# A hybrid attention and RWKV backbone on one core: VectorE's order in the RWKV loop body and the place of SyncE's stores of y

## The chip, the cores and the metric
The program runs on one core of a Trainium2 chip. The metric is device time in microseconds (us) of one execution. The kernel before takes 5541.4 us (median of 3 runs, 5534.21 to 5553.46). All data is float32, but for one small helper product of the attention phase.

## The reference, cut to what matters
The program computes two layers over 2048 latent and 256 context tokens of width 1024. Layer 0 is latent attention beside Fourier mixing, layer 1 is bidirectional RWKV-7 time mixing. The change lies in layer 1 alone, whose recurrence is this (16 heads of 64, two directions `d`):

```
decay = exp(-exp(-softplus(-w_raw) - 0.5));  a = sigmoid(a0 + ad @ a2)
kk = normalised k * k_k;      k_dir = k * (1 + (a - 1) * k_a)
step: sa = S kk;   S = S * decay - sa (kk * a)^T + v k_dir^T;   y = S r
out  = group_norm(y_fwd + y_bwd) + (sum(r * k_dir * r_k)) * v, times a SiLU gate, times w_out
```

The kernel does the recurrence in chunks of 64 tokens. Inside a chunk the steps are a triangular system. Its 64x64 matrix is split in 16x16 blocks: the diagonal blocks are inverted by back substitution, and the rest follows from matrix products.

## The kernel before, in words
`program` runs phases one after the other: modulation, projections, attention, Fourier mixing and their merge (the first 3600 us of the profiled execution), then `rwkv` (L1632 to L2349), then `merge1` with group norm and the output projection.

`rwkv` has 72 items (`NBODY`): 8 pairs of heads times 9 groups of 256 tokens, in this order. One item carries both directions and both heads of a pair, with 4 chunks of 64. The work on an item is spread over six loop bodies, so that one body `n` works on several items at once: the recurrence proper on item n (`step_begin`, `step_sa`, `step_end`, four times), the off-diagonal part of the inverse on item n+1 (`far_p`, `first_order`, `second_w`, `higher_orders`), the inverses' way back from memory on item n+2, scores and block inversion on item n+3, and rates, decays, keys and queries on item n+4, whose inputs are loaded a body earlier. All loops are unrolled. Each engine has its own instruction stream with an order written out by hand in its function `body`; engines meet by semaphores only. An instruction stream stands still at a wait until the semaphore is there, and all that is behind it stands too.

SyncE (SP) issues every DMA of this phase, on one hardware queue. For body n it has in order `store_bonus(n+3)` (2 DMAs), `load(n+5)` (4, and 4 more at the first group of a pair), `keep_products(n+3)` (4 stores of the masked scores), `keep_inverses(n+2)` (1 store of the inverted diagonal blocks), `gather(n+3)` (2 loads of the diagonal blocks of what `keep_products` has stored), `spread(n+2)` (8 loads of the inverses into XB) and `store_y(n)` (4 stores). `gather` waits for the stores of `keep_products` to land; `keep_inverses` waits for GpSimd's last copy; `spread` waits for the store of `keep_inverses` to land.

GpSimd (POOL) has only `invert(n+3)`: one copy into place (L1864), a memset, 28 small multiply and add instructions in a chain (L1870, L1872), four copies out (L1881). It begins when `gather` has landed.

TensorE (PE) begins body n with `bonus(n+3)` (L1915) and runs the four steps of the recurrence with the other products between them. Behind step 2's `step_begin` stand `far_p` (L1957, needs XB from `spread`), `step_sa`, `far_p`, `step_end`, then `first_order` (L1970, needs Pm from VectorE's `blocks`, L2279), step 3 and `higher_orders` (L1988).

VectorE (DVE) runs `bonus`, `decay_of_chunks`, `parameters`, `carry` (L2264) and `decayed` (L2257) for each step, `masks` (L2272), `sums` (L2218 to L2221), `keys` (L2226 to L2230: t1, kd, b0, q), `blocks` (L2279), `add_orders` (L2291), `queries` (L2236, L2237: two products into AR) and `weights` (L2242, L2243: Kc, Bc) in the order of L2303 to L2347. ScalarE copies PSUM results and computes the exponentials; its `take_y` (L2154) writes y into one of two buffers and waits at a body's first step for the stores of two items earlier.

Of the kernel before, what the change touches and what calls it, by code (L numbers as in the profile page):

```python
# [24 lines left out]
ALU = mybir.AluOpType  # L25
# [1606 lines left out]
def rwkv(nc, sem, keep, A, W):  # L1632

    with ExitStack() as stack:
        core = Core(nc, stack, "rw")
        NBODY = PAIRS * NG
# [5 lines left out]
        zin = core.sb("zin", [P, 2, 2, 4, GT])  # L1642
# [3 lines left out]
        cur = core.sb("cur", [P, 7])  # L1646
# [4 lines left out]
        ee = core.sb("ee", [P, 2, 2, GT])  # L1651
        cs, en, t1, kd, b0, q, bv = (core.sb(n, [P, 2, GT]) for n in ("cs", "en", "t1", "kd", "b0", "q", "bv"))
# [28 lines left out]
        ep_done, ar_done, kb_done = (sem(f"rw_{n}") for n in ("ep_en", "ar", "kb"))  # L1681
# [9 lines left out]
        x_mm, x_out, p_mm, p_out, xt_mm, xt_out = ([sem(f"rw_{n}{d}") for d in range(2)] for n in (  # L1691
            "x_mm", "x_out", "p_mm", "p_out", "xt_mm", "xt_out"))
# [31 lines left out]
        def tokens(m, d):  # L1724

            return m.group * GT if d == 0 else ((NG - m.group) % NG) * GT

        def span(first, size):
            return slice(first, first + size) if isinstance(first, int) else bass.ds(first, size)
# [4 lines left out]
        def bodies(one):  # L1734

            for n in range(1 - KEEP - 2, NBODY):
                one(At(n), [0 <= n + k < NBODY for k in range(KEEP + 2)])

        with nc.Block() as block:
            @block.sync  # L1740
            def _(sp):
# [19 lines left out]
                def whole(scratch, d, h, turned=0):  # L1761
                    first = NCH * (4 * turned + 2 * d + h)
                    return W[scratch][first:first + NCH, 0:C * C].rearrange("c (s t) -> s c t", t=C)

                def diagonal(scratch):
                    return W[scratch].rearrange("q (b x) -> (q b) x", b=NSUB)[:, 0:SUB * C].rearrange("u (i t) -> u i t", t=C)[:, :, 0:SUB]
# [21 lines left out]
                def keep_inverses(m):  # L1788

                    sp.wait_ge(inv_done, 4 * m.n + 4)  # L1790
                    if m.since(1):
                        sp.wait_ge(xb_l, 16 * 8 * m.n)
                    sp.dma_start(diagonal("inverses"), g_out[:].rearrange("u (i j) -> u i j", j=SUB)).then_inc(i_st, 16)

                def spread(m):

                    sp.wait_ge(i_st, 16 * (m.n + 1))
                    if m.since(2):
                        for d in range(2):
                            sp.wait_ge(xt_mm[d], 2 * m.n - 3)  # L1800
                    for turned in (1, 0):
                        for d in range(2):
                            for h, (rows, _) in enumerate(HEADS2):
                                sp.dma_start(XB[rows, m.two, turned, d], whole("inverses", d, h, turned)).then_inc(xb_l, 16)

                def store_y(n):
                    sp.wait_ge(y_out, 4 * n.n + 4)
                    for d in range(2):
                        for h, (rows, _) in enumerate(HEADS2):
                            dst = W["y"][d, span(tokens(n, d), GT), span(n.pair * P + HP * h, HP)]  # L1810
                            sp.dma_start(dst.rearrange("(c t) v -> t c v", t=C),
                                         ysb[rows, GT * (2 * n.two + d):GT * (2 * n.two + d) + GT].rearrange("t (c v) -> t c v", c=NCH)).then_inc(y_st[n.two][d], 16)
# [18 lines left out]
                def body(n, has):  # L1831
                    if has[3]:
                        store_bonus(n.on(3))
                    if has[5] and n.since(-3):
                        load(n.on(5))
                    if has[3]:
                        keep_products(n.on(3))
                    if has[2]:
                        keep_inverses(n.on(2))
                    if has[3]:  # L1840
                        gather(n.on(3))
                    if has[2]:
                        spread(n.on(2))
                    if has[0]:
                        store_y(n)

                bodies(body)
                sp.wait_ge(bv_st, 32 * NBODY)
                for both in y_st:
                    for d in range(2):  # L1850
# [344 lines left out]
            def _(v):  # L2195
# [24 lines left out]
                    nc.vector.tensor_tensor_scan(cs[:, 0, :], reset[:, 0, :], ee[:, 0, 0, :], 0.0, ALU.mult, ALU.add).then_inc(cs_done, 1)  # L2220
                    nc.vector.tensor_tensor_scan(cs[:, 1, ::-1], reset[:, 1, ::-1], ee[:, 0, 1, ::-1], 0.0, ALU.mult, ALU.add).then_inc(cs_done, 1)  # L2221

                def keys(m, link):
                    s = m.two
                    v.wait_ge(in_l[s], inputs_loaded(m))
                    link(nc.vector.tensor_scalar(t1[:], ee[:, 1], cur[:, 4:5], cur[:, 5:6], ALU.mult, ALU.add))  # L2226
                    link(nc.vector.tensor_tensor(kd[:], t1[:], zin[:, s, :, 0, :], ALU.mult))
                    link(nc.vector.scalar_tensor_tensor(out=b0[:], in0=ee[:, 1], scalar=-1.0, in1=zin[:, s, :, 1, :], op0=ALU.mult, op1=ALU.mult))
                    v.wait_ge(bon_mm, m.n)
                    nc.vector.scalar_tensor_tensor(out=q[:], in0=zin[:, s, :, 2, :], scalar=cur[:, 6:7], in1=kd[:],  # L2230
                                                   op0=ALU.mult, op1=ALU.mult).then_inc(q_done, 1)

                def queries(m):
                    s = m.two
                    v.wait_ge(ep_done, m.n + 1)
                    nc.vector.tensor_tensor(AR[:, m.six, :, :, 1, :], decayed_to(True), by_chunk(zin[:, s, :, 2, :]), ALU.mult).then_inc(ar_done, 1)  # L2236
                    nc.vector.tensor_tensor(AR[:, m.six, :, :, 0, :], decayed_to(False), by_chunk(zin[:, s, :, 1, :]), ALU.mult).then_inc(ar_done, 1)  # L2237

                def weights(m):

                    v.wait_ge(sc_mm, 4 * m.n)
                    nc.vector.tensor_tensor(Kc[:], kd[:], en[:], ALU.mult)  # L2242
                    nc.vector.tensor_tensor(Bc[:], b0[:], en[:], ALU.mult).then_inc(kb_done, 1)  # L2243
# [38 lines left out]
                def add_orders(m, d, which):  # L2282

                    v.wait_ge(xt_mm[d], 2 * m.n + which + 1)
                    if which == 0:
                        v.wait_ge(xb_l, 16 * 8 * (m.n + 1))
                    else:
                        v.wait_ge(xt_out[d], 2 * m.n + 1)
                    grown = XT[:, m.two, d].rearrange("p c t -> p (c t)")
                    less = grown if which else XB[:, m.two, 0, d].rearrange("p c t -> p (c t)")  # L2290
                    nc.vector.tensor_tensor(grown, bank[XT_AT[d]][:, 0:GT], less, ALU.add).then_inc(xt_out[d], 1)  # L2291
# [11 lines left out]
                def body(n, has):  # L2303
                    m, k, l = n.on(1), n.on(3), n.on(4)
                    link = Link(v, dch, EL * l.n)
                    if has[3]:
                        bonus(k)
                        decay_of_chunks(k)
                    if has[4]:
                        parameters(l)  # L2310
                    if has[0]:
                        carry(n, 0)
                        decayed(n, 1)
                    if has[3]:
                        masks(k, 0, 0)
                    if has[4]:
                        sums(l, link)
                    if has[3]:
                        masks(k, 0, 1)
                    if has[0]:  # L2320
                        carry(n, 1)
                        decayed(n, 2)
                    if has[3]:
                        for d in range(2):
                            masks(k, 1, d)
                    if has[4]:
                        keys(l, link)
                    if has[1]:
                        for d in range(2):
                            blocks(m, d)  # L2330
                    if has[0]:
                        carry(n, 2)
                        decayed(n, 3)
                    if has[1]:
                        for d in range(2):
                            add_orders(m, d, 0)
                    if has[4]:
                        queries(l)
                    if has[0]:
                        carry(n, 3)  # L2340
                        if has[1]:
                            decayed(m, 0)
                    if has[4]:
                        weights(l)
                    if has[1]:
                        for d in range(2):
                            add_orders(m, d, 1)  # L2347

                bodies(body)  # L2349


# [333 lines left out]
```

## Time and profile before
The profiled execution took 5547.19 us, its span in the trace is 5545.2 us.

| what | value |
|---|---|
| median of 3 runs | 5541.4 us |
| profiled execution, own time | 5547.19 us |
| its span | 5545.2 us |
| rwkv phase in it | about 3600 to 5262 us |
| busy over the span, PE / DVE / ACT / POOL | 92% / 50% / 28% / 24% |
| PE busy, 3720 to 5180 us | 1345.54 of 1460 us |
| mean granted TensorE clock | 0.971 of full speed |

A timeline row has the start in us, the duration in us, the engine, the line, the operation with its operands and, in brackets, how long the engine was idle before it and what released it. `SPq` rows are DMA issues: the duration is SP's time for the issue, and not the transfer's. A row with x8 stands for eight instructions in a row.

### The profile page before, as it was taken

The numbers are of one execution on the slowest core, as the hardware profiler recorded it, in microseconds if no ns is written. First come the engines' busy times: TensorE is split into PE (matmuls) and PEld (weight loads), VectorE is DVE, ScalarE is ACT, GpSimd is POOL, SyncE is SP. The second block draws the span as 40 slices with busy tenths as digits, with TensorE's granted clock in tenths as the row PEclk, the third lists the DMA queues.
The fourth block names the chain that finished last, engine by engine and source line by source line (L and its number), as shares of the span: only waits on it lengthen the run. The fifth ranks groups of instructions, "written<-read, shape, count | busy, mean of one in ns | idle before, by whom it ended". The sixth has DMA issues, their size and how long they took to land. (4 is left out here: it accounts for less than half of the span.)

```text
span 5545.2 us, 133161 instructions
## 1 busy us (share of the span) xinstructions
PE 5083.7 (92%) x53870; PEld 3081.3 (56%) x53870; DVE 2745.9 (50%) x4947; ACT 1544.6 (28%) x3503; POOL 1342.8 (24%) x2817
## 2 busy tenths in 40 slices
PE   7899997999999987999999999879999899999879
PEld 2566663333333323444444444468888888888734
DVE  0233343666666651221232222267777666777566
ACT  0111211443434430232211212123333333333222
POOL 0011011222222220000000000045555555555333
PEclk9999997999999998999999999989999999999989
DMA  6212222000000007332121121155555555555485
GB/s 248 74 61 69 64 64 68 4 22 23 22 23 22 22 32 284 123 117 57 57 69 65 57 69 60 50 135 128 131 128 134 129 132 129 132 133 131 86 275 174
DMA packets 926936, 527.19 MB, mean 95 GB/s; under 512 B 661312, under 2 KB 879040, under 8 KB 919360
## 3 DMA queue, kind: packets, MB, share of 16 engines
q1 hardware_dynamic: 926400, 519.62, 33.3%
q8 instruction: 387, 6.34, 0.5%
q14 instruction: 149, 1.22, 0.1%
HBM read 330.98 MB, written 188.49 MB: 94 GB/s over the span
## 5 line engine op out<-in xcount | busy, mean ns | idle before, releaser
L1534 PE MATMUL p_bU<-keep_hT,p_slab 128*128 128x512 f32 (+1 forms) x2592 | 1029.3, 559 | 12.8 <-DMA p_slab<-in_o_w_in_dram 7.3
L1534 PEld LDWEIGHTS p_bU<-keep_hT,p_slab 128*128 128x128 f32 x2592 | 493.4, 191 | 543.6 <-issue 512.1
L883 PE MATMUL at_bS<-at_qT,at_kT 97*64 97x512 f32 (+1 forms) x2368 | 602.4, 598 | 7.2 <-issue 6.6
L1015 DVE TENSOR_REDUCE at_mx<-at_bM 128x1 f32<-128x512 f32 (+1 forms) x656 | 400.6, 629 | 354.0 <-PE at_bM L849 351.0
L978 ACT ACTIVATE at_pT<-at_bS 128x512 f32<-128x512 f32 (+1 forms) x592 | 346.8, 591 | 462.3 <-PE at_bS L883 383.9
L1606 DVE SCALAR_TENSOR_TENSOR p_z<-p_u,p_shift,p_z 128x2306 f32<-128x2306 f32 x26 | 68.2, 2621 | 769.9 <-ACT p_z L1564 769.9
L1872 POOL TENSOR_TENSOR rw_g_at<-rw_g_at,rw_g_prod 64x14 f32<-64x14 f32 (+6 forms) x1008 | 333.4, 331 | 79.0
L1870 POOL TENSOR_TENSOR rw_g_prod<-rw_g_at 64x14 f32<-64x14 f32 (+6 forms) x1008 | 324.4, 322 | 79.1
L2264 DVE SCALAR_TENSOR_TENSOR rw_S<-rw_bank,rw_dec,rw_Sdec 128x64 f32<-128x64 f32 x576 | 136.8, 279 | 382.7 <-PE rw_bank L2039 382.4
L883 PEld LDWEIGHTS at_bS<-at_qT,at_kT 97*64 97x64 f32 x2368 | 161.0, 138 | 267.2 <-issue 214.9
L902 PE MATMUL at_bO<-at_pT,at_va 128*64 128x512 f32 x1152 | 300.5, 600 | 0.0
L806 POOL TENSOR_TENSOR at_sum_pool<-at_sum_pool,at_pT 128x512 f32<-128x512 f32 x128 | 192.8, 1506 | 433.4 <-ACT at_pT L978 422.0
L1036 DVE TENSOR_TENSOR at_sum_vector<-at_sum_vector,at_pT 128x512 f32<-128x512 f32 x320 | 276.1, 863 | 13.1 <-ACT at_pT L978 9.7
L1883 POOL MEMSET rw_zeros<- 128x1040 f32 x1 | 1.0, 964 | 1104.7 <-POOLq L2604 1104.7
L1324 PE MATMUL m_bY<-m_w,m_mT 128*128 128x512 f32 x576 | 251.3, 594 | 0.0
L422 PE MATMUL p_bG<-keep_w_in,p_hT 128*128 128x512 f32 x576 | 250.1, 592 | 0.0
L1558 ACT COPY p_u<-p_bU 128x512 f32<-128x512 f32 (+1 forms) x130 | 69.6, 542 | 643.3 <-PE p_bU L1534 629.3
L849 PE MATMUL at_bM<-at_kTb,at_qTb 96*64 96x512 bf16 (+1 forms) x1312 | 224.5, 365 | 11.9 <-DVE at_mx L1015 10.9
L2495 PE MATMUL m_bY<-m_w,m_oT 128*128 128x512 f32 x512 | 223.5, 595 | 0.0
L373 POOL TENSOR_TENSOR p_hr<-p_hms,p_half 128x8 f32<-128x8 f32 x36 | 58.9, 1636 | 576.6 <-DVE p_hms L558 576.6
L849 PEld LDWEIGHTS at_bM<-at_kTb,at_qTb 96*64 96x64 bf16 x1312 | 75.4, 109 | 219.4 <-issue 136.8
L2154 ACT COPY rw_ysb<-rw_bank 128x128 f32<-128x128 f32 x288 | 77.6, 269 | 387.3 <-DVE rw_S L2264 386.4
(261 smaller groups left out, 9506.2 us busy)
## 6 DMA issues: line engine op xcount, KB each, us to landing
rw_zin<-scratch_heads SPq DMA_DIRECT2D x144, 512.0 KB, 4.7
rw_XB<-scratch_inverses SPq DMA_DIRECT2D x576, 64.0 KB, 2.6
mod_w<-in_ada_w_dram SPq DMA_DIRECT2D x4, 6144.0 KB, 18.1
scratch_heads<-p_z SPq DMA_DIRECT2D x24, 1024.0 KB, 4.9
rw_lin<-scratch_lora SPq DMA_DIRECT2D x144, 128.0 KB, 5.2
scratch_bv<-rw_bv SPq DMA_DIRECT2D x144, 128.0 KB, 2.0
scratch_products<-rw_NB SPq DMA_DIRECT2D x288, 64.0 KB, 4.0
scratch_y<-rw_ysb SPq DMA_DIRECT2D x288, 64.0 KB, 2.2
```

The costliest lines, as they stand in the source:

```text
L422: last = pe.matmul(bG[:, j, :], hT[:, s, k, :], w_in[:, k, E_G0 + 512 * j:E_G0 + 512 * (j + 1)], start=(k == 0), stop=(k == KD - 1))
L849: last = pe.matmul(bM[rows, (FIRST_ITEM[b] + i) % 2, 0:n], qTb[:, s, q0 + VH * x:q0 + VH * x + VH], kTb[:, s, c:c + n], start=True, stop=True)
L883: last = pe.matmul(bS[rows, g % 3, 0:nq * P], kT[:, s, k * P + VH * x:k * P + VH * x + VH], qT[:, s, q0 * P:(q0 + nq) * P], start=True, st ...
L902: last = pe.matmul(out[rows, 0:nq * P], va[:, s, 2 * pair + x, :], pT[:, (g + x) % SLOTS, 0:nq * P], start=(pair == 0), stop=(pair == nk / ...
L978: nc.scalar.activation(pT[:, g % SLOTS, 0:n], bS[:, g % 3, 0:n], ACT.Exp, scale=SCALE).then_inc(exp_done, 1)
L1015: nc.vector.tensor_reduce(mx[:, j, piece:piece + 1], bM[:, (FIRST_ITEM[b] + i) % 2, 0:n], AX.X, ALU.max).then_inc(max_red, 1)
L1036: nc.vector.tensor_tensor(acc, acc, tile, ALU.add).then_inc(added[False], 1)
L1324: last = pe.matmul(bY[:, j, :], mT[:, s, k, :], w[:, k, j * 512:(j + 1) * 512], start=(k == 0), stop=(k == KD - 1))
L1534: last = pe.matmul(bU[:, n % 4, 0:w], slab[:, i, k, :], hT[:, k, tok:tok + w], start=(k == 0), stop=(k == KD - 1))
L1870: link(nc.gpsimd.tensor_tensor(prod, N[:, k + 1:, k:k + 1].broadcast_to([2 * half, rows, k]), N[:, k:k + 1, 0:k].broadcast_to([2 * half, r ...
L1872: link(nc.gpsimd.tensor_tensor(below, below, prod, ALU.add))
L2495: last = pe.matmul(bY[:, 2 * s + j, :], oT[:, s, k, :], w[:, k, j * 512:(j + 1) * 512], start=(k == 0), stop=(k == KD - 1))
```

## The change
On SP, `store_y` of body n's own item at the end of the body becomes `store_y` of the item before, issued between `keep_inverses` and `gather`; one `store_y` for the last item stands behind the loop. `spread` now waits for VectorE's `add_orders` of two items earlier (`xt_out`) where it waited for TensorE's product behind it (`xt_mm`).

On VectorE, `keys` is cut in three. `key_factors` (t1) stays between `masks` and `blocks`. `new_keys` (kd, q) and `bonus_weights` (b0) move behind the first `add_orders`, where `queries` stood. `queries` moves to the end of the body. `weights` waits for `ep_done` itself. No operation is added or taken away.

```diff
@@ SP: spread
-                            sp.wait_ge(xt_mm[d], 2 * m.n - 3)
+                            sp.wait_ge(xt_out[d], 2 * m.n - 3)
@@ SP: body
                         keep_inverses(n.on(2))
+                    if has[0] and n.since(1):
+                        store_y(n.on(-1))
                     if has[3]:
                         gather(n.on(3))
                     if has[2]:
                         spread(n.on(2))
-                    if has[0]:
-                        store_y(n)
 
                 bodies(body)
+                store_y(At(NBODY - 1))
@@ DVE: keys is cut in three
-                def keys(m, link):
+                def key_factors(m, link):
+                    link(nc.vector.tensor_scalar(t1[:], ee[:, 1], cur[:, 4:5], cur[:, 5:6], ALU.mult, ALU.add))
+
+                def new_keys(m, link):
                     s = m.two
                     v.wait_ge(in_l[s], inputs_loaded(m))
-                    link(nc.vector.tensor_scalar(t1[:], ee[:, 1], cur[:, 4:5], cur[:, 5:6], ALU.mult, ALU.add))
                     link(nc.vector.tensor_tensor(kd[:], t1[:], zin[:, s, :, 0, :], ALU.mult))
-                    link(nc.vector.scalar_tensor_tensor(out=b0[:], in0=ee[:, 1], scalar=-1.0, in1=zin[:, s, :, 1, :], op0=ALU.mult, op1=ALU.mult))
                     v.wait_ge(bon_mm, m.n)
                     nc.vector.scalar_tensor_tensor(out=q[:], in0=zin[:, s, :, 2, :], scalar=cur[:, 6:7], in1=kd[:],
                                                    op0=ALU.mult, op1=ALU.mult).then_inc(q_done, 1)
+
+                def bonus_weights(m, link):
+                    s = m.two
+                    link(nc.vector.scalar_tensor_tensor(out=b0[:], in0=ee[:, 1], scalar=-1.0, in1=zin[:, s, :, 1, :], op0=ALU.mult, op1=ALU.mult))
@@ DVE: weights
+                    v.wait_ge(ep_done, m.n + 1)
                     v.wait_ge(sc_mm, 4 * m.n)
@@ DVE: body
                     if has[4]:
-                        keys(l, link)
+                        key_factors(l, link)
                     if has[1]:
                         for d in range(2):
                             blocks(m, d)
...
                     if has[4]:
-                        queries(l)
+                        new_keys(l, link)
+                        bonus_weights(l, link)
                     if has[0]:
                         carry(n, 3)
...
                     if has[1]:
                         for d in range(2):
                             add_orders(m, d, 1)
+                    if has[4]:
+                        queries(l)
```

## Rows read from the trace of the kernel before
**Rows 1.** TensorE's waits, 3720 to 4480 us: line waited for, total us, times, longest
```profile
PE rw_bank L1970 <- DVE rw_Pm L2279: 31.5, 28, 1.5
PE rw_bank L1957 <- DMA rw_XB<-scratch_inverses: 20.1, 14, 3.2
```
**Rows 2.** The same, 4480 to 5180 us
```profile
PE rw_bank L1970 <- DVE rw_Pm L2279: 49.7, 31, 2.2
```
**Rows 3.** The waits of SP's DMA queue, 3720 to 4480 us
```profile
SPq L1786 <- DMA scratch_products<-rw_NB: 76.3, 34, 4.3
SPq L1793 <- POOL rw_g_out L1881: 18.4, 16, 2.6
```
**Rows 4.** Timeline of SP, a late body: from one gather to the next
```profile
4504.54 0.33 SPq L1786 DMA_DIRECT2D rw_g_in<-scratch_products  x1
...
4511.69 3.48 SPq L1811 DMA_DIRECT2D scratch_y<-rw_ysb  x4
...
4519.09 2.62 SPq L1778 DMA_DIRECT2D scratch_products<-rw_NB  x4
4521.81 1.56 SPq L1793 DMA_DIRECT2D scratch_inverses<-rw_g_out  x1
4525.47 0.33 SPq L1786 DMA_DIRECT2D rw_g_in<-scratch_products  x1
```
**Rows 5.** Timeline of SP: the fourth gather of the phase
```profile
3700.34 0.84 SPq L1786 DMA_DIRECT2D rw_g_in<-scratch_products  x1
```
**Rows 6.** Line 1786's instructions: min/median/max ns, first and last start
```profile
L1786 SPq DMA_DIRECT2D rw_g_in<-scratch_products x72: 325/332/1189, 3642.8 to 5209.5; - x72
```
**Rows 7.** POOL by line, 3720 to 4480 us: busy us, mean ns, idle before
```profile
L1864 POOL COPY rw_g_at<-rw_g_in 32x256 f32<-32x256 f32 x34 | 14.3, 421 | 236.1 <-DMA rw_g_at<-scratch_products 236.1
```
**Rows 8.** The same, 4480 to 5180 us
```profile
L1864 POOL COPY rw_g_at<-rw_g_in 32x256 f32<-32x256 f32 x32 | 15.2, 475 | 263.1 <-DMA rw_g_at<-scratch_products 263.1
```
**Rows 9.** Timeline, the late body of rows 4: POOL, one VectorE scan, TensorE's far_p
```profile
4507.67 0.39 POOL L1864 COPY rw_g_at<-rw_g_in 32x256 f32<-32x256 f32 x1 [8.19 <-DMA rw_g_at<-scratch_products]
...
4514.46 0.27 POOL L1870 TENSOR_TENSOR rw_g_prod<-rw_g_at 64x50 f32<-64x50 f32 x1
...
4514.81 0.61 POOL L1872 TENSOR_TENSOR rw_g_at<-rw_g_at,rw_g_prod 64x50 f32<-64x50 f32 x1
...
4515.32 0.69 DVE L2220 TENSOR_TENSOR_SCAN rw_cs<-rw_reset,rw_ee 128x256 f32<-128x256 f32 x1
...
4518.59 2.27 POOL L1881 COPY rw_g_out<-rw_g_at 32x256 f32<-32x256 f32 x4
...
4519.33 0.60 PEld L1957 LDWEIGHTS rw_bank<-rw_XB,rw_NB 64*64 64x64 f32 x16
```
**Rows 10.** Timeline of SP, an early body: gather, stores of y
```profile
4279.36 0.33 SPq L1786 DMA_DIRECT2D rw_g_in<-scratch_products  x1
...
4287.74 2.59 SPq L1811 DMA_DIRECT2D scratch_y<-rw_ysb  x4
...
4299.73 0.38 SPq L1793 DMA_DIRECT2D scratch_inverses<-rw_g_out  x1
4301.52 0.78 SPq L1786 DMA_DIRECT2D rw_g_in<-scratch_products  x1
```
**Rows 11.** Timeline of POOL, the same body
```profile
4283.30 0.39 POOL L1864 COPY rw_g_at<-rw_g_in 32x256 f32<-32x256 f32 x1 [7.63 <-DMA rw_g_at<-scratch_products]
...
4296.81 2.90 POOL L1881 COPY rw_g_out<-rw_g_at 32x256 f32<-32x256 f32 x4
```
**Rows 12.** Timeline, TensorE's far_p in that body
```profile
4289.47 0.68 PE L1957 MATMUL rw_bank<-rw_XB,rw_NB 64*64 64x64 f32 x16 [0.73 <-DMA rw_XB<-scratch_inverses]
```
**Rows 13.** Timeline of VectorE, the first of blocks in the late body
```profile
4522.83 0.75 DVE L2279 TENSOR_TENSOR rw_Pm<-rw_bank,rw_far 128x256 f32<-128x256 f32 x2
```
**Rows 14.** Timeline of TensorE, from first_order to the next body's begin
```profile
4501.20 1.15 PE L1970 MATMUL rw_bank<-rw_XB,rw_Pm 64*64 64x64 f32 x32 [1.98 <-DVE rw_Pm L2279]
...
4506.20 1.13 PE L1915 MATMUL rw_bank<-rw_q,rw_same 128*128 128x512 f32 x2
```

## The prediction
> **What bounds the kernel now.** I read the share of busy time first, and it misleads: TensorE is busy 92% of the span, and in the stretch 3720 to 5180 us, which is the steady part of the RWKV loop, 1345.54 of 1460 us. A reader would take the loop as bound by TensorE with some 8% of idle time. So the second view is TensorE's waits in that stretch. Two lines hold nearly all of them: `first_order` (L1970) waits for VectorE's Pm, 31.5 + 49.7 us, and `far_p` (L1957) waits for the DMA that brings XB, 20.1 us [rows 1, 2]. Together 101.3 us over some 66 bodies, 1.53 us each.
>
> The third view is SP's own timeline, since XB comes from there. How long is a body? The 72 gathers run from 3642.8 to 5209.5 us [rows 6]; from the fourth, at 3700.34 us [rows 5], to the last are 68 bodies in 1509.2 us: 22.19 us each. In one such body, from 4504.54 to 4525.47 us, SP issues back to back: stores of y end where those of the bonus begin, and so on to the products, which end at 4521.71. Only in front of `gather` does it stand still, after the store of the inverses [rows 4]. The waits of SP's queue say so too: 76.3 us in 34 bodies, 2.24 each, for the stored products to land, and GpSimd's result is late in 16 of the 34, 18.4 us in all [rows 3]. So SP itself is almost full, and it is a second bound at about TensorE's period.
>
> The fourth view is GpSimd, whose 24% of busy time looks harmless. It is one link of a ring that nothing can pipeline: gather(n+3) lands, GpSimd inverts, SP stores the result, and only then SP issues the next gather, since the order on SP says so. In the late body gather is issued at 4504.54, GpSimd starts at 4507.67 and ends at 4520.86 (4518.59 + 2.27): 3.13 us and then 13.19 us [rows 4, 9]. In an early body it starts at 4283.30, 3.94 us behind the gather of 4279.36, and ends at 4299.71: 16.41 us for the same 35 instructions; SP stores at 4299.73, 0.02 us later [rows 10, 11]. By groups, GpSimd's idle time in front of its first copy is 236.1/34 = 6.9 us a body in the early stretch and 263.1/32 = 8.2 us in the late one [rows 7, 8]; with 760/34 and 700/32 us for a body it works 15.4 and 13.7 us.
>
> **Why GpSimd's time varies.** One small multiply of 64x50 takes 0.27 us, the add of the same shape begun 0.35 us later takes 0.61 us, and a scan of VectorE over operands in SBUF runs from 4515.32 for 0.69 us at the same time as GpSimd's next ones [rows 9]. Over the trace, GpSimd's instructions stretch while VectorE runs operations whose operands all lie in SBUF (`sums`, t1, kd, b0, q, Kc, Bc, both of AR, `decayed`) and not while VectorE reads PSUM (`masks`, `blocks`, `carry`, `add_orders`). In GpSimd's stretch of the late body I count 4.0 us of such VectorE work (the first in it is `decayed` at 4512.73, the last kd, cut off at 4520.86), in that of the early body 8.6 us (from L2218 at 4283.66 to Bc at 4297.67, 15 instructions). So (16.41 - 13.19)/(8.6 - 4.0) = 0.70 us of GpSimd per us of it. What sets the count is the phase: `far_p` starts 14.8 us behind the gather in the late body (4519.33) and 10.1 us in the early one (4289.47), where TensorE had waited 0.73 us for XB [rows 9, 12].
>
> **The change part by part.**
> (a) *VectorE, keys behind blocks.* In the late body `blocks` starts at 4522.83, 3.5 us behind `far_p` [rows 9, 13], because kd, b0 and q stand ahead of it. In the new order t1 is over 1.05 us behind the start of `far_p`, `blocks` follows, and the first Pm is there before `step_end`, so TensorE's 31.5 + 49.7 us go [rows 1, 2]: up to 81.2/66 = 1.23 us a body. What is late next: the second product of `far_p` and `step_end`, which run to 2.0 us behind `far_p`'s start; nothing in between waits for VectorE.
> (b) *kd, q, b0 in the place of queries.* Three operations of about 0.7 us for two (the scan of 0.69 us is the nearest size [rows 9]): 0.8 us more in front of the fourth `carry`. There VectorE had been idle 1.3 to 2.4 us for TensorE's last product of the step; I charge 0, and if that cover fails 0.3 us a body.
> (c) *queries last.* Its 1.4 us now stand in front of the next body's `bonus`, where VectorE had waited 3.2 us ahead of the first `carry`. AR and bv are wanted 6.6 us into the body; ScalarE's `rates` wants AR 5.5 us in, and it is there some 3.5 us in. Cost 0, upper end 0.3 us.
> (d) *The two waits.* `weights` waits for exponentials that are more than 5 us old; `spread` for sums a body old. Behind `spread`'s wait on SP stand only the next body's issues. 0.
> (e) *Stores of y on SP.* 3.48 us of issue in the late body, 2.59 in the early one [rows 4, 10]; I take 3.1 with 0.1 between. They fill the 2.24 us in front of `gather` and also the 0.5 us in which `spread` waited. SP's own sum falls from 22.2 to about 19.5 us. But they now stand in GpSimd's ring: between the inverses' store and the gather. `take_y` wants y of two items before; in the tight phase that lands about when it is asked for, some 0.6 us late at worst, under TensorE's wait for XB.
>
> Three periods are left. TensorE: 22.19 - 1.53 = 20.7 us; the sum of one body is the same, 5.0 us from `first_order` to the next body [rows 14], 13.1 from there to `far_p` [rows 9, 14] and 2.0 back to `first_order`: 20.1 at full clock. SP: 19.5. The ring: 3.3 (gather to GpSimd's start; 3.13 and 3.94 above) + P + 0.03 + 0.4 (store of inverses) + 3.2 (y) = 6.9 + P. P depends on the phase. At the start `far_p` is 14 us behind the gather: queries have left GpSimd's stretch, so P is about 14.0 and the ring 20.9, plus 0.2 for a worse landing: 21.1. That is longer than TensorE's 20.7, so TensorE gains on the ring and `far_p` moves towards the gather, which brings kd, q, b0 and both weights into GpSimd's stretch. It stops where TensorE waits for XB, 9 to 10 us behind the gather. There the stretch holds half of `sums` (1.0 us), t1 0.6, kd, q, b0 2.2, Kc and Bc 1.4, a part of queries 0.4 and three `decayed` 0.9: 6.5 us, P = 13.19 + 0.70 x (6.5 - 4.0) = 14.9, and the ring 22.0 with 0.2 for the landing. So in the end the loop runs at the ring's pace, 0.2 us under today's. I give the drift 16 bodies: 16 x (22.19 - 21.1) = 17 us and 52 x (22.19 - 22.0) = 10 us. Sum: -27 us. The profiled execution's own time, 5547.19, would be 5520; it lies 5.8 us above the median of 5541.4, so against that I forecast **5514 us**. P has ends of 13.2 and 16.4 from rows 9 and 11, the issue of y 2.6 and 3.5 from rows 10 and 4: rings of 19.7 to 23.9.
>
> The Trainium skill, SBUF — State Buffer, section "SBUF: two separate sides", says that a VectorE operation with two inputs in SBUF and a GpSimd operation that reads SBUF exclude each other for a whole instruction and do not share bandwidth. The two bodies agree in kind (0.27 against 0.61 us), with 0.70 us lost per us of overlap. It speaks against this change, because it lets the ring grow where one counts SP's time alone: with a full 1.0 us per us, P would be 15.7 and the steady ring 22.8 us, slower than today's.
>
> **The rivals.**
> *Ring too long (slower).* The place is SP between the inverses' store and `gather`; the price is y's issue plus a GpSimd that is stretched more than by my count, or a gather that lands behind y's packets. It decides from P + landing over 18.6 us. For it: P of 16.4 was seen at just this phase [rows 11]. Against: queries, 1.4 us, have left that stretch. With P at 15.9 and 22.9 us for 60 bodies: 60 x 0.75 - 8 x 1.1 = +36, so 5577 us.
> *TensorE's pace (faster by more).* The ring stays near its short phase, with P at 13.5 to 13.8. For it: the late stretch keeps 13.7 us for 32 bodies [rows 8], and any lull of TensorE's clock moves the phase back. Against: the ring's 21.1 is then still longer than 20.7 by my count. 20.8 us for 68 bodies: -95, so 5446 us.
> *Nothing to be had.* The ring in its locked phase has just today's period, and the short phase lasts few bodies: 5541 us. That SP is nearly full today could be a follower's slack and no bound; then only the ring's 22.2 counts.
>
> **How the numbers follow.** Forecast 0.43, its own range 5490 to 5540; ring too long 0.23; TensorE's pace 0.18; nothing 0.16. About 0.3%, 17 us, is what a measurement of this kernel can tell from no change: under 5525 the forecast's case has two thirds of its chance (0.29) and TensorE's pace all of it, which gives 0.48 for faster; the rest of the forecast's (0.12) and of the third rival's (0.14) give 0.26 for the same, 0.26 is slower. The range of 5452 to 5580 leaves out somewhat more than half of the lower case and under half of the upper one.
>
> **What would show it.** Right: TensorE's wait of L1970 for Pm is gone; a wait of L1957 for XB stands in most bodies from the middle of the loop on, about 1 us each; SP waits for GpSimd (L1793) in nearly every body and for the products in hardly any; the gather follows the stores of y at once; GpSimd works about 15 us a body and idles 7. Wrong: L1793's wait stays rare and L1957's absent (then TensorE sets the pace, near 5446), or bodies of more than 22.5 us with GpSimd above 15.5 us (the slower case); a Pm wait that stays, or a new wait of TensorE for AR, Kc or q, would refute (a), (b) or (c).

## The result: slower by 0.5%, and the profile after
The changed kernel takes 5566.9 us (median of 6 runs, 5560.4 to 5570.3) against 5538.9 us before; the ratio is 1.005, with a 95% interval of 1.0039 to 1.0061. The forecast was 5514. The profiled execution took 5566.7 us, its span is 5564.7 us, and from the fourth gather (3700.05 us) to the last (5229.7 us) it is 1529.7 us where it was 1509.2: these 68 bodies are 20 us longer, about the whole of the difference. Of the rivals it is the slower one, "ring too long".

TensorE's waits of the kernel after, 3720 to 4480 us (answers to [rows 1]):
```profile
PE rw_bank L1958 <- DMA rw_XB<-scratch_inverses: 27.0, 22, 2.2
PE rw_bank L2011 <- ACT rw_ysb L2155: 21.3, 13, 2.6
```
The wait for Pm (31.5 us) is gone, as part (a) had it, and nothing was won: TensorE waits for XB instead, and for ScalarE's copy of y, which stands still until the stores of y two items earlier have landed (34.3 us in 17 of ScalarE's waits in this stretch).

SP's waits in the same stretch (to [rows 3]):
```profile
SPq L1793 <- POOL rw_g_out L1882: 97.3, 30, 5.2
SPq L1811 <- ACT rw_ysb L2155: 4.8, 5, 2.1
```
The 76.3 us for the stored products are gone too. SP now waits for GpSimd in 30 of 34 bodies where it did in 16. An engine that waits is no bound, so SP has been relieved, and the ring with GpSimd in it sets the pace. The second row is no wait: at the store issued at 4329.62 us, one of these five, ScalarE's last copy of that y had ended at 4305.95; the issue itself took so long. One turn of the ring, SP (to [rows 4, 10]):
```profile
4288.79 0.55 SPq L1786 DMA_DIRECT2D rw_g_in<-scratch_products  x1
...
4300.27 2.66 SPq L1778 DMA_DIRECT2D scratch_products<-rw_NB  x4
4308.24 0.38 SPq L1793 DMA_DIRECT2D scratch_inverses<-rw_g_out  x1
4308.66 3.61 SPq L1811 DMA_DIRECT2D scratch_y<-rw_ysb  x4
4312.37 0.55 SPq L1786 DMA_DIRECT2D rw_g_in<-scratch_products  x1
```
and GpSimd and TensorE in it (to [rows 11, 12]):
```profile
4292.91 0.39 POOL L1865 COPY rw_g_at<-rw_g_in 32x256 f32<-32x256 f32 x1 [8.38 <-DMA rw_g_at<-scratch_products]
...
4305.12 3.09 POOL L1882 COPY rw_g_out<-rw_g_at 32x256 f32<-32x256 f32 x4
```
```profile
4298.74 0.68 PE L1958 MATMUL rw_bank<-rw_XB,rw_NB 64*64 64x64 f32 x16
```
SP has its products out at 4302.93 and stands until 4308.24. Landing 4.12, GpSimd 15.30, wake-up 0.03, store of the inverses 0.38, y and its gaps 3.75: 23.58 us, one of the longer turns. `far_p` starts 9.95 us behind the gather.

The same sum can be drawn up for every kernel below. These are means over the gathers 5 to 70 of each profiled execution, in us: the period from gather to gather; gather to GpSimd's start; GpSimd's work P; from its end to the issue of the inverses' store; that issue; from there to the next gather; and how far `far_p` starts behind the gather.

```
kernel                          period landing    P   to SP  issue  to gather  far_p behind
before                           22.19   3.27  14.67   1.22   0.60     2.42        13.7
changed                          22.53   3.67  14.61   0.06   0.41     3.78        10.1
VectorE's order alone            21.88   3.20  14.81   0.93   0.59     2.34         9.9
SP's order alone (at 5608 us)    23.16   3.65  15.38   0.06   0.38     3.69        10.0
y ahead of the inverses          21.35   4.36  14.28   1.93   0.64     0.13        12.6
pad in SBUF                      22.72   3.77  14.78   0.07   0.41     3.68        10.0
pad with PSUM                    22.41   3.62  14.39   0.15   0.42     3.83        10.4
y split around gather            21.41   3.69  14.14   0.28   0.53     2.78        12.8
y ahead, bonus behind gather     20.73   4.48  13.92   1.49   0.68     0.15        15.6
products ahead of load           23.17   7.09  13.68   1.76   0.54     0.11        17.0
that of 20.73, VectorE's old     21.94   4.27  13.96   2.92   0.68     0.11        18.5
```
"To SP" tells ring from SP: near 0.03 us SP stood waiting for GpSimd and the ring is the bound; above a microsecond GpSimd was done and SP was busy, or stood, with something else. The row of SP's order alone is of an execution of 5608 us, and of that kernel more is said below. A ratio counts only the executions within 1.5% of the fastest of their kernel, which leaves out four of SP's order alone, all above 5600 us.

Against the kernel before GpSimd's own time is the same (14.61 and 14.67). What grew is the way from the inverses' store to `gather`, 1.36 us, where y's issue stands in place of the wait for the products, and the landing, 0.40 us; the 1.22 us of slack behind GpSimd's end is used up.

### The profile page after: what moved, and what is told of

It is laid out like the page before. It is cut to its first block and busy times, and to the rows that moved or that the text cites. A ratio compares the mean times of both kernels' runs of the same rounds, so it can differ in the third digit from the quotient of the medians.

```text
span 5564.7 us, 133236 instructions
## 1 busy us (share of the span) xinstructions
PE 5090.7 (91%) x53870; PEld 3083.8 (55%) x53870; DVE 2762.1 (50%) x4947; ACT 1545.1 (28%) x3503; POOL 1337.0 (24%) x2817
## 5 line engine op out<-in xcount | busy, mean ns | idle before, releaser
L1871 POOL TENSOR_TENSOR rw_g_prod<-rw_g_at 64x14 f32<-64x14 f32 (+6 forms) x1008 | 308.1, 306 | 79.1
L1882 POOL COPY rw_g_out<-rw_g_at 32x256 f32<-32x256 f32 x288 | 192.9, 670 | 17.8
## 6 DMA issues: line engine op xcount, KB each, us to landing
mod_w<-in_ada_w_dram SPq DMA_DIRECT2D x4, 6144.0 KB, 18.3
```

Of the source, the lines that this page charges most:

```text
L1871: link(nc.gpsimd.tensor_tensor(prod, N[:, k + 1:, k:k + 1].broadcast_to([2 * half, rows, k]), N[:, k:k + 1, 0:k].broadcast_to([2 * half, r ...
```

## The experiments
**Either part alone.** First the diff's VectorE part with the old SP order, then SP's part with VectorE's old order.

> VectorE's new order alone; on SP the stores of y stay at the end of the body. Ring theory (the new order on SP puts the issue of y into the ring gather, GpSimd, store of the inverses, next gather): without y the ring is about 18.5 us a body and no bound; SP, full at 22.2 us before, keeps its sum, so the time stays within 0.4% of before (5520 to 5555), TensorE's waits move from L1970 (Pm) to L1958 (XB). Rival, VectorE's order is what costs: slower than before by the 0.5% of the change, some 5565. Rival, TensorE was the bound: 1.2 us a body less, 5455.

Measured: 5525.8 us, 0.9972 of before (0.996 to 0.9983). The waits of TensorE are for XB, as expected (3720 to 5180 us):
```profile
PE rw_bank L1957 <- DMA rw_XB<-scratch_inverses: 73.2, 49, 3.5
```
VectorE's order is not what costs, and TensorE was not the bound: with Pm's wait gone SP's turn, its waits for its own stores in it, sets the pace, at 21.88 us. `far_p` is 9.9 us behind the gather here too, and GpSimd is no faster than in the changed kernel (14.81 us): the tight phase costs little as long as y is out of the ring.

> SP's new order alone; VectorE keeps the old one, with keys ahead of blocks and queries ahead of the fourth carry. Ring theory: slower than before, and by more than the whole change, since queries (1.4 us of VectorE work in SBUF) lie in GpSimd's stretch too: GpSimd 15 to 15.5 us a body, period 23.0, 5580 to 5610. Rival, VectorE's order is what costs: about 5540 or faster.

> The kernel with SP's new order alone once more, for another profile: in five of its seven executions it took 5523 to 5530 us, in two 5608 and 5611, and the profiled one was of the second kind (far_p 10.0 us behind gather, GpSimd 15.4 us a body). Phase theory: an execution of the first kind has far_p 12 us or more behind gather, GpSimd below 14.7 us, TensorE waiting for Pm rather than for XB, and a period of about 22.0. Rival, the second kind is a disturbance from outside: the same phase and the same GpSimd time, with other stretches (PE clock, DMA landing) longer.

> The kernel with SP's new order alone, timed again. Two levels were seen, 5525 and 5610 us. If they are two phases of one ring in which an execution settles by itself, both come again in some mixture and hardly anything between; the profiled one shows far_p 10 us behind gather if it is near 5610, and 12 us or more if it is near 5525. If the first series' 5525 was chance, all are near 5610.

The first expectation was missed in five executions of seven, and what came is the best view of the mechanism. The first series had executions of 5523 to 5530 us (five) and of 5608 and 5611; the ratio of the five is 0.9967 (0.9955 to 0.998). The profiled one is that of 5608 us, and it is as expected: GpSimd 15.38 us, period 23.16. The second time the one execution took 5616, with `far_p` 10.2 us behind the gather, GpSimd 15.43 us and a period of 23.21: the same again. The third series had 5522, 5529, 5530, 5533, 5535, 5569, 5583, 5586, 5622 and 5623 us; without the last two the ratio is 0.9989 (0.9964 to 1.0015), no change that this can tell. Low and high times come again, but three lie between, and the trace of one of these says why. The granted clock does not tell them apart (0.971 at 5530 and 5586 us, 0.970 and 0.971 at 5608 and 5611). In the profiled one of 5586 us the phase changes half-way. Its gather of 3803.98 us and the `far_p` behind it:
```profile
3803.98 0.60 SPq L1786 DMA_DIRECT2D rw_g_in<-scratch_products  x1
```
```profile
3821.60 0.68 PE L1958 MATMUL rw_bank<-rw_XB,rw_NB 64*64 64x64 f32 x16
```
17.6 us. The gather of 4285.00 us and its `far_p`:
```profile
4285.00 0.55 SPq L1786 DMA_DIRECT2D rw_g_in<-scratch_products  x1
```
```profile
4294.22 0.68 PE L1958 MATMUL rw_bank<-rw_XB,rw_NB 64*64 64x64 f32 x16 [0.27 <-DMA rw_XB<-scratch_inverses]
```
9.2 us, and TensorE waited for XB, where in the first part it had waited for Pm. TensorE's waits, 3720 to 3960 us:
```profile
PE rw_bank L1971 <- DVE rw_Pm L2280: 16.2, 11, 1.8
```
Over the bodies 5 to 18 the period is 22.17 us with P 14.02 and `far_p` 16.6 us behind; between the gathers of 3892 and 4075 us the distance falls from 17.4 to 10.0; over the bodies 25 to 70 the period is 23.05, P 15.37 and the distance 10.0. Landing (3.45 and 3.67) and the way to `gather` (3.85 and 3.60) hardly differ, so it is GpSimd's time that makes the ring longer. The VectorE work with two SBUF inputs inside GpSimd's stretch is 3.7 us in the first part and 6.6 in the second. One program, one execution, two speeds of GpSimd, and they go with the phase; in this trace the tight phase stays once it is reached. That the executions of 5522 to 5535 us are loose throughout fits, but none of them was profiled. What tips an execution over was not tested; at the beginning of this fall stand a way to `gather` of 5.7 us and one of 4.1.

**y out of the ring.** The changed kernel with two lines of SP's body in the other order.
```diff
+                    if has[0] and n.since(1):
+                        store_y(n.on(-1))
                     if has[2]:
                         keep_inverses(n.on(2))
-                    if has[0] and n.since(1):
-                        store_y(n.on(-1))
```


> The changed kernel with the stores of y issued between the stores of the products and the store of the inverses, and so outside of the ring, in time in which SP waits for GpSimd. Ring theory: ring 3.5 + 14.3 + 0.5 = 18.4 us, SP some 19.5, TensorE 20.7 to 21 sets the pace: 5440 to 5470 us. Rival, the stores of y hurt wherever they come before gather (their packets delay it): 5540 or more. Rival, VectorE's order costs: no better than 5540.

Measured: 5489.0 us, 0.9901 (0.9887 to 0.9915). The ring is loosened and the time falls by 78 us against the changed kernel, but stays 19 us above the upper end of the expectation. "To SP" is 1.93 us: SP is the bound again, and its waits (3720 to 5180 us) name the new one:
```profile
SPq L1804 <- DMA scratch_inverses<-rw_g_out: 93.0, 69, 2.7
```
The wait that y had covered in front of `gather` comes back in front of `spread`, since `gather` now follows the inverses' store at once.

**Half of y out of the ring.** Direction 0 is stored ahead of `gather`, direction 1 behind it.

> The changed kernel with the stores of y cut in two: direction 0 (2 DMAs) ahead of gather, direction 1 behind it and ahead of spread. The same issues, half of them taken out of the ring. Theory A (ring, priced by the SP time between the store of the inverses and gather, 3.78 us in the changed kernel): that falls by 1.8 us, and the period from 22.5 to 21 or less, where TensorE or SP itself takes over: 5440 to 5480. Theory B (what makes the changed kernel slow is the phase, with far_p 10 us behind gather, and not the place of y): it stays above 5540.

Measured: 5496.5 us, 0.9922 (0.9909 to 0.9936). Theory B is out, for 1.00 us less between the inverses' store and `gather` shortened the period by 1.12 us. The gain in SP's time is 1.0 us and not 1.8, because the stores are not equal: the first of the four, directly behind the inverses' store, takes 1.39 us in the changed kernel and 1.80 here, each of the others 0.65 to 0.78, and the first is in the half that stayed in the ring.

**The wait in front of spread covered as well.** The kernel with y ahead, its bonus stores moved.
```diff
                     if m.since(2):
+                        sp.wait_ge(bv_done, m.n - 1)
...
-                    if has[3]:
-                        store_bonus(n.on(3))
...
                         gather(n.on(3))
+                        store_bonus(n.on(3))
```


> The kernel of 5489 us (y between products and inverses) with the two stores of the bonus moved between gather and spread, where SP waits 1.35 us a body for the inverses' store to land; load waits for the bonus product itself. If SP is the bound of that kernel (its ring has 1.9 us of slack): period from 21.35 to about 20.8, then TensorE's pace, 5445 to 5470. If TensorE or the XB transfer sets its pace: 5480 to 5495, no change.

Measured: 5444.3 us, 0.9827 (0.9811 to 0.9843), just below the lower end of the expectation, and the best kernel of this study. The period is 20.73 us, the 20.7 that the prediction had for TensorE alone, and TensorE is busy for 1344.51 of the 1380 us from 3720 to 5100 (97%, 92% before). SP's turn in it:
```profile
4358.13 0.96 SPq L1794 DMA_DIRECT2D scratch_inverses<-rw_g_out  x1
4359.93 0.65 SPq L1787 DMA_DIRECT2D rw_g_in<-scratch_products  x1
4360.62 0.48 SPq L1787 DMA_DIRECT2D rw_g_at<-scratch_products  x1
```
`far_p` is 15.6 us behind the gather and P is 13.92 us.

> SP's order of the kernel of 5444 us (y ahead of the inverses, bonus behind gather), with VectorE's old order. What VectorE's order is worth once SP is out of the way: if TensorE sets the pace there, its waits for Pm come back, 1.2 us a body, and 68 bodies make 80 us: 5515 to 5535. If VectorE's order never mattered, 5444. If the old order also brings GpSimd back over the bound (queries in its stretch), above 5540.

Measured: 5524.6 us, 0.996 (0.9947 to 0.9974). TensorE's waits (3720 to 5100 us):
```profile
PE rw_bank L1971 <- DVE rw_Pm L2280: 93.4, 62, 2.0
```
and SP's:
```profile
SPq L1777 <- DVE rw_NB L2273: 57.8, 44, 2.8
SPq L1779 <- DVE rw_NB L2273: 54.3, 53, 1.8
```
VectorE's order is worth 80 us where SP and the ring leave room (5524.6 against 5444.3, two series; by the ratios 1.3%, 74 us), and 18 us (0.28%) where SP is full. The 2.92 us "to SP" of this kernel are not SP's own work alone: it stands for 112 us in this stretch in front of the products' stores, which wait for VectorE's masks.

**Load as the cover.**

> The changed kernel with another order on SP: bonus, products, load, inverses, gather, y, spread, so that load covers the products' landing and y the inverses'. y is out of the ring, but gather's packets stand behind load's 1.3 MB: landing some 6 us where it was 3.7. Ring 6 + 13.9 + 0.6 = 20.5, TensorE 20.8: 5440 to 5480. If load's packets delay gather by 4 us or more: 5500 to 5540.

Measured: 5608.0 us, 1.0111 (1.0095 to 1.0126), worse than every case expected:
```profile
4445.76 0.54 SPq L1793 DMA_DIRECT2D scratch_inverses<-rw_g_out  x1
4446.40 3.34 SPq L1786 DMA_DIRECT2D rw_g_in<-scratch_products  x1
```
Behind load's transfers the issue itself takes 3.34 us here and 4.21 in the mean, where 0.37 was the mean before, so the landing term is 7.09 us. SP hardly stands any more: its issues alone are 21.7 us a body (18.3 in the changed kernel), and SP, not the ring, is the bound. P, with `far_p` 17.0 us behind, is the shortest of all.

**GpSimd beside VectorE.** Two additions of 128x256 ahead of the first `add_orders` of the changed kernel; in the twin one operand is the PSUM bank.
```diff
+                    if which == 0:
+                        nc.vector.tensor_tensor(pad[:, 2 * m.two + d], less, less, ALU.add)
```


> The changed kernel with two more VectorE additions of 128x256 a body, ahead of the first add_orders, with both operands in SBUF and their result unused. They lie in GpSimd's stretch. Theory of the shared SBUF access: 0.84 us more VectorE work in SBUF stretches GpSimd by 0.4 to 0.6 us a body, and since the ring sets the pace, the time grows by 30 to 40 us over the changed kernel, to about 5600. Rival, GpSimd's stretching is only a matter of phase or of DMA: same as the twin with a PSUM operand, 5565 to 5575.

> The twin of the kernel before it: the same two additions at the same place with one operand in PSUM. VectorE is as busy, GpSimd is left alone: 5565 to 5575 by the theory of the shared access. If VectorE's length alone mattered, both twins would be equal.

Measured: 5578.3 us, 1.0058 (1.0041 to 1.0075), and 5566.7 us, 1.0035 (1.0023 to 1.0046). GpSimd by line, the SBUF pad first, then the PSUM pad (3720 to 5180 us):
```profile
L1874 POOL TENSOR_TENSOR rw_g_at<-rw_g_at,rw_g_prod 64x14 f32<-64x14 f32 (+6 forms) x896 | 282.6, 315 | 70.2
L1872 POOL TENSOR_TENSOR rw_g_prod<-rw_g_at 64x14 f32<-64x14 f32 (+6 forms) x896 | 273.4, 305 | 70.3
```
```profile
L1874 POOL TENSOR_TENSOR rw_g_at<-rw_g_at,rw_g_prod 64x14 f32<-64x14 f32 (+6 forms) x910 | 279.3, 307 | 71.3
L1872 POOL TENSOR_TENSOR rw_g_prod<-rw_g_at 64x14 f32<-64x14 f32 (+6 forms) x910 | 268.3, 295 | 71.4
```
The sign is right and the size a third of the expectation: 12 us between the twins where some 30 were expected, and their intervals overlap by a hair. P differs by 0.39 us for 0.90 us of VectorE work (two of 0.45; 0.41 each in the PSUM twin), 0.43 us per us. But against the changed kernel the SBUF pad adds only 0.17 us to P and the PSUM pad takes 0.22 from it, with `far_p` 10.4 us behind instead of 10.0, and why is open. So the times alone do not prove that VectorE's SBUF work stretches GpSimd.

The trace of the kernel before shows it instruction by instruction (3720 to 5180 us). Take each of GpSimd's small multiplies and adds as a multiple of the fastest tenth of its own line and shape. Beside no VectorE work at all the mean is 1.01 (481 of them); beside `masks` into NB alone, which reads PSUM, 1.01 (179); beside `carry` alone, PSUM too, 1.00 (145); beside `queries` alone, two SBUF inputs, 2.47 (12), and beside q alone 2.51 (5). Counted by bodies, P is about 11.8 us plus 0.59 us for each us of VectorE work with two SBUF inputs in the stretch (an estimate by a straight line through 66 bodies; since a longer stretch also takes in more of that work, it is rather high). The kernels agree: 3.3 us of such work and P 13.92 with bonus behind `gather`, 5.1 and 14.61 in the changed kernel, 6.5 and 15.38 with SP's order alone at 5608 us.

## Why the prediction was wrong
Its mechanism was right: the ring is the bound of the changed kernel, SP waits for GpSimd in nearly every body, the wait for Pm is gone, `far_p` settles at about 10 us behind the gather. The sum failed at two terms, and with them the sign: a ring of 22.0 us is faster than the 22.19 before, one of 22.5 is slower.

1. *The ring in its tight phase: 22.0 forecast, 22.53 measured.* "3.2 (y)" was 3.78. I had taken y's issue from where it stood before, where the four stores take 3.17 us with their gaps; behind the inverses' store they take 3.63, and 0.15 more stand around them. The excess is in the first store: 1.39 us in the mean where it was 0.81, and the other three are as before. The landing was 3.67 where 3.5 was reckoned, wake-up and store 0.47 where 0.43; P was 14.61 where 14.9 was. So P erred to the other side, by 0.3 us.
2. *"I give the drift 16 bodies" at 21.1 us.* There was no drift, because there was no distance to lose: `far_p` is 11.2 us behind the second gather, 11.7 behind the fourth and 10.1 behind the fifth, where the kernel before has 14.7 and 13.8 at the fourth and fifth. The bodies of the first 16 gathers after the fourth take 22.65 us each (3722.81 to 4085.20 us). The 21.1 also had the loose ring from terms that were too small: with the measured ones it is 3.67 + 14.0 + 0.47 + 3.78 = 21.9 us (an estimate with P as in the loose part of the execution of 5586 us).

By size: 16 x 1.55 = 25 us for the drift and 52 x 0.44 = 23 us for the tight phase (its later bodies take 22.44) are the 48 us between -27 and the +20 of the profiled execution.

The reading of the kernel before also needs a word. "SP is almost full" holds: with TensorE's waits for Pm gone the time fell by 0.28% only. VectorE's order alone gained 0.3%, SP's alone 0.3% in its low executions and nothing over all of the third series, and both together lost 0.5%. The account that fits: VectorE's order removes the wait for Pm that had kept TensorE, and so VectorE's SBUF work, away from GpSimd's stretch, and SP's order lengthens the ring just where GpSimd is slow. In the tight phase VectorE's order by itself helps even then, for it takes `queries` out of that stretch (P 14.61 against 15.38 and a period of 22.53 against 23.16 with SP's order alone at 5608 us). The prediction had both halves, and sized their meeting too small. Charging (b), (c) and (d) nothing was right: no wait for q, Kc or AR is among TensorE's nine longest kinds of wait from 3720 to 5180 us. Small slips moved nothing: GpSimd has 34 instructions a body and not 35, the early body's SBUF work is 14 rows and not 15, and the ends of the ring, 19.7 and 23.9, come out as 19.8 and 23.9 with the 0.2 for the landing. The late landing of y, put at "some 0.6 us late at worst, under TensorE's wait for XB", did show as a wait of its own, 21.3 us in 34 bodies.

## What to carry to other kernels
Look for rings before filling a stall: an in-order queue that issues both a transfer and, behind the answer to it, the next one has a loop length, and any issue put between the two is in it, however idle the queue is elsewhere. Put the filler where the queue waits for somebody else's work (here ahead of the inverses' store), and then look at which wait is next; two moves of this kind (y and the bonus) made 1.7% together with VectorE's new order, and 0.4% without it. Two edits that gain alone can lose together when one moves the phase that the other's price depends on. And a kernel that ran at one level in one profile may run at another in the next execution: look at all the times before reading the one trace.

## What the runs showed of the hardware that was not expected
- SP's time for the same DMA issue depends on what was issued ahead: the first store of y 0.69 us at the end of the body (VectorE's order alone), 1.39 directly behind the inverses' store, 1.80 there in the split, with the other three at 0.64 to 0.78 in all of them; the gather's first load 0.37, 1.22 directly behind the inverses' store, 4.21 with load's transfers ahead too.
- GpSimd's same 34 instructions take 13.7 to 15.4 us in the mean of a kernel, by how much of VectorE's work with two SBUF inputs falls beside them (2.8 to 6.5 us).
- The phase of two engines can differ between executions of one program, and change within one: with SP's order alone they run from 5522 to 5623 us, at a granted clock of 0.969 to 0.972.
